# Scan stage of a hybrid decoder layer: the old sample states turned and multiplied ahead of the unit loop

## Chip, cores and metric

One core of one Trainium2 chip runs the whole layer in one launch. The metric is the device time of one execution in microseconds; given is the median of three runs. The instructions are put on five engines by hand: TensorE (PE), VectorE (DVE), ScalarE (ACT), GpSimd (POOL) and SyncE (SP), which here issues the loads and stores of the stage. Each engine works through its own list in order and waits on semaphores.

## What is computed

A layer over one prompt of 512 tokens and eight samples of 8 tokens each: latent attention, a state-space scan, a merge, and a mixture of experts. The change is in the scan. Of the reference:

```python
a_cs = jnp.cumsum(dt * a, axis=2)
cb = jnp.einsum('bclgn,bcsgn->bclsg', cm, bm)
w_ls = cb[..., None] * decay_ls * dt[:, :, None]
y_diag = jnp.einsum('bclsgh,bcsghp->bclghp', w_ls, x)
states = jnp.einsum('bclgn,bclgh,bclghp->bcghpn', bm, decay_end * dt, x)
def step(h, inp):
    s_c, d_c = inp
    return d_c[..., None, None] * h + s_c, h
y_off = jnp.einsum('bclgn,bcghpn->bclghp', cm, h_prev) * jnp.exp(a_cs)[..., None]
```

The prompt starts from a zero state; each sample starts from its own old state (32 heads of 64 by 128 numbers), which gives a part of its outputs (`y_off`), is aged by the decay over its 8 tokens, and gets a new part added (`states`). Everything is float32.

## The kernel before

The scan, `stage_ssd`, stands between the convolution and the merge; stages end in a barrier of all engines. It has G = 4 groups of 8 heads (512 columns, GW) and in each group NT = 5 units: four of 128 prompt tokens, the fifth with all 64 sample tokens. That makes N = 20 units k = 5g + i.

Ahead of the loop come the step sizes and decays (VectorE and ScalarE, L1595 to L1633), their cumulative sums on TensorE (L1397 to L1403), and a round trip of rows through device memory (L1341, L1342), from which `decays(k)` (L1326) loads the rows that unit k needs, three units ahead.

TensorE's list in turn k of the loop (L1515) is: `inputs(k)` (transposes L1417, then b and c.b, L1423 and L1424), `gate(k-1)` (eight products of 128x512 with the z weights, L1443), `turn(k-2)` (transposes of a finished y, L1512), `outputs(k-1)` (eight head products L1455, the product with the prompt's state L1458, the new state L1461). VectorE's list in its turn k is: copy b, mask c.b, subtract (L1654), minimum (L1656), after ScalarE's exponential the product L1659; then for unit j = k-1 the scaling L1670, three sums and products into y, the prompt state's update (L1685, L1687), and the norm (L1704).

In a sample unit `outputs` has more. After transposing the finished prompt state (L1466), it takes the eight old states of the group in h0 (128 x 4 x 8 x 128) one by one: four transposes (L1480), ScalarE's copy to h0T (L1582), a product (L1489) of 64 masked columns c_of with it, all into PSUM bank 5, while VectorE ages h0 (L1668). Then eight products (L1498) of 64 rows make the new parts in two banks in turn, and VectorE adds each to h0 (L1694) before its bank is used again. The masked operands are made by GpSimd (L1386, L1389). SP loads h0 of a group with four transfers of 512 KB (L1320), stores it with four (L1334), and loads the next group's only when the stores have landed. It does so in one list with the decay rows, the z weights (L1315) and the norm's gains (L1337).

## Time and profile before

| | us |
|---|---|
| runs: median (lowest to highest) | 2748.0 (2741.38 to 2751.46) |
| profiled execution, device time | 2731.32 |
| profiled execution, span of the trace | 2729.6 |
| busy over the span: TensorE | 2533.2 (93%) |
| VectorE | 1860.1 (68%) |
| ScalarE | 1345.2 (49%) |
| GpSimd | 482.8 (18%) |
| mean granted TensorE clock | 0.955 of full speed |

Busy times are those of the profiled execution, in which matmul ends are modelled. Work is named by the line of the kernel that issues it. A float32 product stands in the trace as two records, and a transpose as one. PEclk is the share of full speed that was granted: 1.00 is 2.4 GHz, 0.50 is 1.2 GHz. In brackets behind a row of a timeline stands how long the engine had been idle, and what released it.

### The profile page before, as it was taken

The page shows a single profiled execution, that of the slowest core. Times are in us where ns is not written, and L with a number is a line of the kernel's source. Part 1 is how long each engine was busy: PE and PEld are TensorE (multiplying, and loading weights), DVE is VectorE, ACT ScalarE, POOL GpSimd, SP SyncE. Part 2 cuts the span into 40 slices and gives each one's busy share as a digit, 9 for nine tenths or more (in the row PEclk, how much of TensorE's full clock was granted, in tenths as well). Part 3 has the DMA queues.
Part 4 walks back from the last instruction along what each step waited for, and adds up shares of the span by engine and source line. Part 5 has one row for each costly group of instructions (what it writes and reads, how often), then busy time and mean ns, then how long its engine had stood idle before and what let it go on. Part 6 is the DMA issues. An engine that isn't in the chain of part 4 may idle for free. (4 is left out here: it accounts for less than half of the span.)

```text
span 2729.6 us, 35842 instructions
## 1 busy us (share of the span) xinstructions
PE 2533.2 (93%) x13071; PEld 1934.0 (71%) x13071; DVE 1860.1 (68%) x2181; ACT 1345.2 (49%) x1412; POOL 482.8 (18%) x332
## 2 busy tenths in 40 slices
PE   8798999798995999979978899999999999999996
PEld 5355555598993444439976788888888888888882
DVE  0344444333775666653456799999999999999996
ACT  0243323132333454433122577777777777777771
POOL 0001122000001333210010721122222222122220
PEclk9899999899997898889988999999999999999998
DMA  4102344132214124213250899999999999999985
GB/s 145 69 1 99 117 157 171 35 93 68 78 62 140 58 94 131 83 50 86 84 200 27 302 408 401 384 379 386 383 378 381 378 380 377 380 384 378 379 338 197
DMA packets 239605, 589.63 MB, mean 216 GB/s; under 512 B 21680, under 2 KB 110992, under 8 KB 235024
## 3 DMA queue, kind: packets, MB, share of 16 engines
q1 hardware_dynamic: 222328, 512.09, 51.7%
q0 software_dynamic: 17168, 76.05, 7.3%
q8 instruction: 73, 1.20, 0.2%
q14 instruction: 36, 0.29, 0.0%
HBM read 555.18 MB, written 32.78 MB: 215 GB/s over the span
## 5 line engine op out<-in xcount | busy, mean ns | idle before, releaser
L2419 DVE TENSOR_TENSOR w_lo<-w_raw,w_hi 128x2048 fp32r<-128x2048 f32 x291 | 664.2, 2293 | 64.7 <-ACT w_hi L2372 63.0
L2372 ACT ACTIVATE w_hi<-w_raw 128x2048 fp32r<-128x2048 f32 x288 | 552.3, 1918 | 144.7 <-PE banks L2291 117.5
L2291 PE MATMUL banks<-w_hi,x_hi 128*128 128x512 f32 x1024 | 320.0, 394 | 3.6 <-DVEq L2458 2.0
L2291 PE MATMUL banks<-w_lo,x_hi 128*128 128x512 f32 x1024 | 316.9, 391 | 0.0
L2291 PE MATMUL banks<-w_hi,x_lo 128*128 128x512 f32 x1024 | 316.1, 390 | 0.0
L2419 DVE TENSOR_TENSOR w_lo<-mergedT,w_hi 128x2048 fp32r<-128x2048 f32 x96 | 220.7, 2299 | 23.1 <-ACT w_hi L2372 23.1
L2291 PEld LDWEIGHTS banks<-w_hi,x_lo 128*128 128x128 f32 x1024 | 192.8, 188 | 41.0
L2291 PEld LDWEIGHTS banks<-w_lo,x_hi 128*128 128x128 f32 x1024 | 192.9, 188 | 40.7
L2291 PEld LDWEIGHTS banks<-w_hi,x_hi 128*128 128x128 f32 x1024 | 190.5, 189 | 41.9 <-DVEq L2458 2.0
L2372 ACT ACTIVATE w_hi<-mergedT 128x2048 fp32r<-128x2048 f32 x96 | 184.1, 1918 | 49.1 <-PE banks L2291 42.7
L2250 POOL DMA_INDIRECT y_rows<-xT,to_row x33 | 52.3, 1585 | 818.9 <-ACT xT L2402 817.7
L2291 PE MATMUL banks<-w_hi,h_hi 128*128 128x512 f32 x512 | 158.3, 390 | 0.0
L2291 PE MATMUL banks<-w_hi,h_lo 128*128 128x512 f32 x512 | 158.0, 390 | 0.0
L2291 PE MATMUL banks<-w_lo,h_hi 128*128 128x512 f32 x512 | 157.8, 389 | 0.0
L1443 PE MATMUL banks<-wz,xT 128*128 128x512 f32 (+1 forms) x320 | 144.8, 606 | 1.5 <-ACT zs L1558 1.5
L2291 PEld LDWEIGHTS banks<-w_hi,h_hi 128*128 128x128 f32 x512 | 96.0, 188 | 20.9 <-DVE h_lo L2423 0.4
L2291 PEld LDWEIGHTS banks<-w_lo,h_hi 128*128 128x128 f32 x512 | 96.1, 188 | 20.6
L1443 PEld LDWEIGHTS banks<-wz,xT 128*128 128x128 f32 (+1 forms) x320 | 57.5, 185 | 74.9 <-issue 74.4
L2291 PEld LDWEIGHTS banks<-w_hi,h_lo 128*128 128x128 f32 x512 | 96.1, 188 | 20.2
L1381 POOL TENSOR_TENSOR xdt<-xs_t,dt 128x512 f32<-128x512 f32 (+1 forms) x20 | 26.1, 1303 | 420.8 <-ACT xs_t L1548 420.8
L1025 PE MATMUL banks_a<-part_hi_a,w_mhi_a 128*128 128x288 f32 x384 | 83.2, 298 | 14.2 <-DVE w_mlo_a L1061 14.2
L2236 POOL DMA_INDIRECT xT<-h_rows,from_row x32 | 83.8, 2619 | 28.6 <-POOL from_row L2232 27.8
(469 smaller groups left out, 4762.3 us busy)
## 6 DMA issues: line engine op xcount, KB each, us to landing
w_raw<-in_exp_w_gu SPq DMA_DIRECT2D x196, 1024.0 KB, 7.6
w_raw<-in_exp_w_down SPq DMA_DIRECT2D x96, 1024.0 KB, 5.9
mergedT<-in_exp_w_gu SPq DMA_DIRECT2D x64, 1024.0 KB, 7.4
mergedT<-in_exp_w_down SPq DMA_DIRECT2D x32, 1024.0 KB, 6.6
w_x<-in_w_in SPq DMA_DIRECT2D x11, 1024.0 KB, 5.2
out<-h SPq DMA_DIRECT2D x20, 512.0 KB, 4.7
wz<-in_w_in SPq DMA_DIRECT2D x4, 2048.0 KB, 10.4
dec<-acs_rows SPq DMA_DIRECT2D x16, 512.0 KB, 3.9
```

The lines of the kernel that those rows point to most:

```text
L1025: mm = pe.matmul(bank_of(u)[:, piece], wp[:, u % NW, k, :], part[:, piece * H2:(piece + 1) * H2], start=(k == 0 and wp is w_hi and n == 0) ...
L1381: ins = pool.tensor_tensor(heads(o[0:n, k % 2], n), x, f[:, g * HG:(g + 1) * HG].unsqueeze(2).broadcast_to((n, HG, PD)), ALU.mult)
L1443: mm = pe.matmul(banks[0:n, 7, :], sb.xT[:, q, P * i:P * i + n], wz[:, g % 2, q, :], start=(q == 0), stop=(q == KD - 1))
L2236: pool.indirect_dma_start(out=x_raw, out_offset=None, in_=io.h_rows, in_offset=bass.IndirectOffsetOnAxis(ap=from_row[:, par, :].bitcast(U3 ...
L2250: pool.indirect_dma_start(out=io.y_rows, out_offset=bass.IndirectOffsetOnAxis(ap=to_row[:, par, :].bitcast(U32), axis=0), in_=y_out, in_of ...
L2291: mm = pe.matmul(banks[:, bank + c, :], x[:, k, :], part[:, s % NHI, j, c * 512:(c + 1) * 512], start=start, stop=last)
L2372: act.activation(w_hi[:, s % NHI], raw(s, par), ACT.Copy).then_inc(hi_ready, 1)
L2419: dve.tensor_tensor(w_lo[:, s % NHI], raw(s, par), w_hi[:, s % NHI].bitcast(F32), ALU.subtract).then_inc(lo_ready, 1)
```

## The change

All 32 old states are now loaded once ahead of the unit loop, by halves of a group (`half_states`, four transfers of 256 KB each) that alternate between the two halves of h0, in front of, between and behind the loads that SP had there. TensorE takes them in 16 pairs: `turn_pair` transposes two samples' states into two banks, ScalarE (`old_copy`) and VectorE (`old_put`) copy one each, and `old_outputs` multiplies them with the masked c: the first sample of a pair goes to PSUM partitions 0 to 63, the second to 64 to 127, summed over the four pairs of a group. ScalarE copies the upper half out and VectorE adds both into old_y. The cumulative sums (`decay_sums`) come after the eighth pair. `seq_decays` makes the 32 heads' sample decays in one go after the first inputs; they were made per group (L1430, L1646).

The group's h0 is loaded a second time for the new states, as before. Its ageing is four instructions over 128x1024, two in the third and two in the fourth unit of the group, ahead of that unit's y; old_y is scaled in the fourth. The eight new-state products stand one behind each of the eight gate products of the sample unit, with 32 rows each: b_of has half its width, and the two halves of the rows hold samples 0 to 3 and 4 to 7. They go to banks 2 and 3. VectorE's additions (`add_new`) stand behind the next unit's minimum, or at the start of the last turn. The sample unit's `outputs` is left with its head products and the transposes of the prompt state. Buffers: h0T now lies in xdt and xend, c_of has two buffers, old_y is new. Each diff line below is cut from the full diff, whose renamings and semaphore counts are left out.

```diff
+        t1, t2, t3 = (y[:, 0, j * NT * SH:(j + 1) * NT * SH].rearrange("p (i h) -> p i h", i=NT) for j in range(3))
+        h0T = [t[:, j, :] for t in (xdt, xend) for j in range(2)]
+        uppers = [zs[0:NS, :], off[0:NS, :]]
+        old_y = buf("old_y", [NS, G, GW])
...
-        c_of = buf("c_of", [P, NSEQ, NS])
-        b_of = buf("b_of", [NS, NSEQ, NST])
-        e_seq = buf("e_seq", [P, 4, NSEQ])
+        c_ofs = [buf(f"c_of{j}", [P, NSEQ, NS]) for j in range(2)]
+        b_of = c_ofs[1][0:NS].rearrange("p b n -> p (b n)").rearrange("p (b n) -> p b n", b=NSEQ // 2)
+        e_seq = buf("e_seq", [P, G, 4, NSEQ])
...
+                def last_state(g):
                     sp.wait_ge(fin_out, g + 1)
                     sp.dma_start(io.o_ssmp[g * GW:(g + 1) * GW, :].rearrange("(q p) n -> p q n", p=P), st_out[:]).then_inc(p_out, 16)
+
+                def new_states(g):
                     sp.wait_ge(hs_out, 8 * (g + 1))
...
+                def half_states(c):
+                    g, half = divmod(c, 2)
+                    if c >= 2:
+                        sp.wait_ge(hT_ready, 2 * (c - 1))
+                    for q in range(4):
+                        at = g * GW + q * P
+                        sp.dma_start(h0[:, q, 4 * half:4 * half + 4], io.ssm[4 * half:4 * half + 4, at:at + P, :].rearrange("b p n -> p b n")).then_inc(half_in[half], 16)
+
+                for c in range(2):
+                    half_states(c)
                 z_weights(0)
+                for c in range(2, 6):
+                    half_states(c)
                 sp.wait_ge(rows_out, 1)
                 sp.dma_start(io.acs_rows[0:4 * SH, :], acsT[:, 0, :]).then_inc(rows_in, 16)
                 sp.dma_start(io.acs_rows[4 * SH:5 * SH, 0:NS], acsT[0:SH, 1, 0:NS]).then_inc(rows_in, 16)
                 sp.wait_ge(rows_in, 32)
                 for k in range(3):
                     decays(k)
+                for c in range(6, 8):
+                    half_states(c)
                 z_weights(1)
+                sp.wait_ge(hT_ready, NP)
                 old_states(0)
...
             def _(pool):
+                for g in range(G):
+                    if g >= 2:
+                        pool.wait_ge(off_part, PAIRS * (g - 1))
+                    pool.tensor_tensor(c_ofs[g % 2][:], sb.xbcT[:, 20 + g, SEQ:T].unsqueeze(1).broadcast_to((P, NSEQ, NS)),
+                                       K[:, K_BCOL:K_BCOL + NSEQ * NS].rearrange("p (b n) -> p b n", b=NSEQ), ALU.mult).then_inc(c_put, 1)
...
                     if i == NT - 1:
                         if g >= 1:
                             pool.wait_ge(hs_ready, 8 * g)
-                        pool.tensor_tensor(c_of[:], sb.xbcT[:, 20 + g, SEQ:T].unsqueeze(1).broadcast_to((P, NSEQ, NS)),
-                                           K[:, K_BCOL:K_BCOL + NSEQ * NS].rearrange("p (b n) -> p b n", b=NSEQ), ALU.mult)
                         pool.wait_ge(cb_out, k + 1)
-                        pool.tensor_tensor(b_of[:], b_t[0:NS, k % 2, :].unsqueeze(1).broadcast_to((NS, NSEQ, NST)),
-                                           K[0:NS, K_BROW:K_BROW + NSEQ].unsqueeze(2).broadcast_to((NS, NSEQ, NST)), ALU.mult).then_inc(of_seq, 1)
+                        many = (NS, NSEQ // 2, NST)
+                        pool.tensor_tensor(b_of, b_t[0:NS, k % 2, :].unsqueeze(1).broadcast_to(many),
+                                           K[0:NS, K_BROW:K_BROW + NSEQ // 2].unsqueeze(2).broadcast_to(many), ALU.mult).then_inc(of_seq, 1)
...
+                def seq_decays():
+
+                    pe.wait_ge(prep_a, 4)
+                    for h in range(SH):
+                        q, half = h // 2, PD * (h % 2)
+                        e_h = e_end[0:NS, NT - 1, h:h + 1].broadcast_to((NS, PD))
+                        mm = pe.matmul(banks[half:half + PD, 3, q * NSEQ:(q + 1) * NSEQ], e_h,
+                                       K[0:NS, K_BEND:K_BEND + NSEQ], start=True, stop=True)
+                    mm.then_inc(e_ready, 1)
...
+                def turn_pair(v):
+
+                    g, p = divmod(v, PAIRS)
+                    pe.wait_ge(half_in[v // 2 % 2], 64 * (v // 4 + 1))
+                    if v >= 2:
+                        pe.wait_ge(hT_out, v - 1)
+                        pe.wait_ge(hT_put, v - 1)
+                    for j in range(2):
+                        for q in range(4):
+                            mm = pe.transpose(banks[:, TURN + 2 * (v % 2) + j, q * P:(q + 1) * P], h0[:, q, 2 * p + j, :], K[:, K_ID:K_ID + P])
+                    mm.then_inc(hT_ready, 1)
...
+                def old_outputs(v):
+
+                    g, p = divmod(v, PAIRS)
+                    pe.wait_ge(hT_out, v + 1)
+                    pe.wait_ge(hT_put, v + 1)
+                    if p == 0:
+                        pe.wait_ge(c_put, g + 1)
+                        if g >= 2:
+                            pe.wait_ge(old_sum, g - 1)
+                    for j in range(2):
+                        mm = pe.matmul(banks[j * NS:(j + 1) * NS, SUM + g % 2, :], c_ofs[g % 2][:, 2 * p + j, :], h0T[2 * (v % 2) + j],
+                                       start=(p == 0), stop=(p == PAIRS - 1))
+                    mm.then_inc(off_part, 1)
...
+                def new_states(g, u):
+
+                    q, half = divmod(u, 2)
+                    if u == 0:
+                        pe.wait_ge(of_seq, g + 1)
+                        pe.wait_ge(e_out, 1)
+                    if 8 * g + u >= 2:
+                        pe.wait_ge(hs_out, 8 * g + u - 1)
+                    k = NT * g + NT - 1
+                    rows = slice(32 * half, 32 * half + 32)
+                    pe.matmul(banks[:, 2 + half, :], xend[rows, k % 2, q * P:(q + 1) * P], b_of[rows], start=True, stop=True).then_inc(hs_ready, 1)
...
-                    if g >= 1 and i == 0:
-                        pe.wait_ge(hs_out, 8 * g)
+                    else:
+                        pe.wait_ge(old_sum, G)
                     for q in range(KD):
                         mm = pe.matmul(banks[0:n, 7, :], sb.xT[:, q, P * i:P * i + n], wz[:, g % 2, q, :], start=(q == 0), stop=(q == KD - 1))
-                    mm.then_inc(z_ready, 1)
+                        if q == KD - 1:
+                            mm.then_inc(z_ready, 1)
+                        if i == NT - 1:
+                            new_states(g, q)
...
                         if g >= 1 and i == 0:
-                            pe.wait_ge(hs_out, 8 * g)
+                            pe.wait_ge(fin_out, g)
...
+                    mm.then_inc(y_ready, 1)
                     pe.wait_ge(st_new, NT * (g + 1))
                     for q in range(4):
                         mm = pe.transpose(banks[:, 6, q * P:(q + 1) * P], stT[:, q * P:(q + 1) * P], K[:, K_ID:K_ID + P])
                     mm.then_inc(fin_ready, 1)
-                    pe.wait_ge(h_in, 64 * (g + 1))
-                    pe.wait_ge(of_seq, g + 1)
...
-                    turn_state(0)
-                    for b in range(NSEQ):
-                        m = NSEQ * g + b
-                        if b + 1 < NSEQ:
-                            turn_state(b + 1)
-                        pe.wait_ge(hT_out, m + 1)
-                        mm = pe.matmul(banks[0:n, 5, :], c_of[:, b, :], h0T[:, b % 2, :], start=(b == 0), stop=(b == NSEQ - 1))
-                        mm.then_inc(off_part, 1)
-                        if b == NSEQ - 1:
-                            pe.wait_ge(off_part, m + 1)
-                            pe.sem_inc(y_ready, 1)
-                    for u in range(8):
-                        q, half = divmod(u, 2)
-                        if u >= 2:
-                            pe.wait_ge(hs_out, 8 * g + u - 1)
-                        mm = pe.matmul(banks[:, 6 + u % 2, :], xend[0:n, k % 2, q * P:(q + 1) * P], b_of[:, 4 * half:4 * half + 4, :],
-                                       start=True, stop=True)
-                        mm.then_inc(hs_ready, 1)
-                    pe.wait_ge(hs_ready, 8 * g + 8)
-                    pe.sem_inc(st_ready, 1)
...
+                def decay_sums():
+
+                    pe.wait_ge(prep_v, 6)
...
+                    mm.then_inc(sums_ready, 1)
+
+                turn_pair(0)
+                for v in range(NP):
+                    if v + 1 < NP:
+                        turn_pair(v + 1)
+                    old_outputs(v)
+                    if v == NP // 2 - 1:
+                        decay_sums()
+                pe.wait_ge(sums_out, 1)
+                pe.wait_ge(rows_out, 1)
...
+                def old_copy(v):
+
+                    act.wait_ge(hT_ready, v + 1)
+                    if v >= 2:
+                        act.wait_ge(off_part, v - 1)
+                    act.activation(h0T[2 * (v % 2)], banks[:, TURN + 2 * (v % 2), :], ACT.Copy).then_inc(hT_out, 1)
+                    if v >= 1 and v % PAIRS == 0:
+                        upper_half(v // PAIRS - 1)
+
+                def upper_half(g):
+
+                    act.wait_ge(off_part, PAIRS * (g + 1))
+                    if g >= 2:
+                        act.wait_ge(old_sum, g - 1)
+                    act.activation(uppers[g % 2], banks[NS:2 * NS, SUM + g % 2, :], ACT.Copy).then_inc(half_out, 1)
...
+                for v in range(NP // 2 + 1):
+                    old_copy(v)
...
+                for v in range(NP // 2 + 1, NP):
+                    old_copy(v)
+                upper_half(G - 1)
...
-                            for b in range(NSEQ):
-                                m = NSEQ * g + b
-                                act.wait_ge(hT_ready, m + 1)
-                                if m >= 2:
-                                    act.wait_ge(off_part, m - 1)
-                                act.activation(h0T[:, b % 2, :], banks[:, 7 - b % 2, :], ACT.Copy).then_inc(hT_out, 1)
...
+                def add_new(g):
+
+                    dve.wait_ge(aged, 2 * (g + 1))
+                    for u in range(8):
+                        q, half = divmod(u, 2)
+                        dve.wait_ge(hs_ready, 8 * g + u + 1)
+                        old = h0[:, q, 4 * half:4 * half + 4, :].rearrange("p b n -> p (b n)")
+                        dve.tensor_tensor(old, old, banks[:, 2 + half, :], ALU.add).then_inc(hs_out, 1)
+
+                def old_put(v):
+
+                    dve.wait_ge(hT_ready, v + 1)
+                    if v >= 2:
+                        dve.wait_ge(off_part, v - 1)
+                    dve.tensor_copy(h0T[2 * (v % 2) + 1], banks[:, TURN + 2 * (v % 2) + 1, :]).then_inc(hT_put, 1)
+                    if v >= 1 and v % PAIRS == 0:
+                        add_halves(v // PAIRS - 1)
+
+                def add_halves(g):
+
+                    dve.wait_ge(half_out, g + 1)
+                    dve.tensor_tensor(old_y[:, g, :], uppers[g % 2], banks[0:NS, SUM + g % 2, :], ALU.add).then_inc(old_sum, 1)
...
+                for v in range(NP // 2 + 1):
+                    old_put(v)
...
+                for v in range(NP // 2 + 1, NP):
+                    old_put(v)
+                add_halves(G - 1)
...
                         dve.tensor_scalar(seg, seg, 0.0, None, ALU.min).then_inc(seg_out, 1)
+                        if k >= 1 and unit(k - 1)[1] == NT - 1:
+                            add_new(unit(k - 1)[0])
...
+                        if k == 0:
+                            dve.wait_ge(e_ready, 1)
+                            dve.tensor_copy(e_seq[:].rearrange("p g q b -> p (g q b)"), banks[:, 3, 0:G * 4 * NSEQ]).then_inc(e_out, 1)
+                            dve.wait_ge(e_out, 1)
+                    else:
+                        add_new(G - 1)
...
                         hs = slice(g * HG, (g + 1) * HG)
-                        if i == NT - 1:
-                            for b in range(NSEQ):
-                                dve.wait_ge(hT_ready, NSEQ * g + b + 1)
-                                dve.tensor_tensor(h0[:, :, b, :], h0[:, :, b, :], e_seq[:, :, b:b + 1].broadcast_to((P, 4, NST)), ALU.mult).then_inc(aged, 1)
+                        if i in (2, 3):
+                            dve.wait_ge(h_in, 64 * (g + 1))
+                            for q in (2 * (i - 2), 2 * (i - 2) + 1):
+                                ins = dve.tensor_tensor(h0[:, q], h0[:, q], e_seq[:, g, q].unsqueeze(2).broadcast_to((P, NSEQ, NST)), ALU.mult)
+                            ins.then_inc(aged, 1)
+                        if i == NT - 2:
+                            dve.wait_ge(old_sum, G)
+                            dve.tensor_tensor(heads(old_y[:, g, :], NS), heads(old_y[:, g, :], NS), e_acs[0:NS, NT - 1, hs].unsqueeze(2).broadcast_to((NS, HG, PD)),
+                                              ALU.mult).then_inc(old_scaled, 1)
                         dve.wait_ge(y_ready, j + 1)
-                        dve.tensor_tensor(heads(off[0:n], n), heads(banks[0:n, 5, :], n), e_acs[0:n, i, hs].unsqueeze(2).broadcast_to((n, HG, PD)),
-                                          ALU.mult).then_inc(y_step, 1)
-                        dve.wait_ge(y_step, 2 * j + 1)
+                        if i < NT - 1:
+                            dve.tensor_tensor(heads(off[0:n], n), heads(banks[0:n, 5, :], n), e_acs[0:n, i, hs].unsqueeze(2).broadcast_to((n, HG, PD)),
+                                              ALU.mult).then_inc(y_step, 1)
+                            dve.wait_ge(y_step, 2 * j + 1)
+                            earlier = off[0:n]
+                        else:
+                            dve.wait_ge(old_scaled, g + 1)
+                            dve.sem_inc(y_step, 1)
+                            earlier = old_y[:, g, :]
...
-                        else:
-                            for u in range(8):
-                                q, half = divmod(u, 2)
-                                dve.wait_ge(hs_ready, 8 * g + u + 1)
-                                old = h0[:, q, 4 * half:4 * half + 4, :].rearrange("p b n -> p (b n)")
-                                dve.wait_ge(aged, NSEQ * (g + 1))
-                                ins = dve.tensor_tensor(old, old, banks[:, 6 + u % 2, :], ALU.add)
-                                ins.then_inc(hs_out, 1)
-                            if g + 1 < G:
-                                dve.memset(stT[:], 0.0).then_inc(st_new, 1)
+                        elif g + 1 < G:
+                            dve.wait_ge(fin_ready, g + 1)
+                            dve.memset(stT[:], 0.0).then_inc(st_new, 1)
```

## Rows read from the trace of the kernel before

**Rows 1.** Table of stretches: length, busy us (count) by engine, PEclk, DMA share, GB/s.

```profile
1009.00:1022.00 13.00, 12.63 (x48) 4.88 (x48) 5.54 (x8) 5.44 (x10) 0.00 (x0) 1.00 0.00 0
1026.00:1036.00 10.00, 10.00 (x12) 3.14 (x10) 3.48 (x6) 0.90 (x1) 0.00 (x0) 0.50 0.01 2
1136.00:1144.00 8.00, 8.00 (x40) 5.15 (x40) 4.12 (x7) 2.51 (x5) 0.00 (x0) 1.00 1.06 296
524.00:538.00 14.00, 13.22 (x61) 13.03 (x62) 2.73 (x8) 0.00 (x0) 0.00 (x0) 0.50 0.00 0
834.00:1223.00 389.00, 346.06 (x1290) 173.37 (x1290) 235.11 (x365) 169.60 (x245) 102.72 (x68) 0.89 0.31 94
```

**Rows 2.** Timeline of PE, second group's sample turn and first's: start, us, operation [idle before].

```profile
906.07 0.60 PE L1417 MATMUL banks<-const,xbcT 128*128 128x128 f32 x4
...
946.75 1.09 PE L1417 MATMUL banks<-const,xbcT 128*128 128x128 f32 x4 [0.30 <-PE banks L1498]
...
985.45 0.63 PE L1430 MATMUL banks<-const,e_end 64*64 64x8 f32 x16
...
996.93 0.60 PE L1417 MATMUL banks<-const,xbcT 128*128 128x128 f32 x4
...
997.79 7.08 PE L1443 MATMUL banks<-wz,xT 128*64 128x512 f32 x16
...
1006.46 0.66 PE L1466 MATMUL banks<-const,stT 128*128 128x128 f32 x4
...
1017.78 0.66 PE L1480 MATMUL banks<-const,h 128*128 128x128 f32 x4
...
1018.37 1.07 PE L1489 MATMUL banks<-h0T,c_of 128*64 128x512 f32 x2
...
1019.37 0.66 PE L1480 MATMUL banks<-const,h 128*128 128x128 f32 x4
...
1025.50 10.60 PE L1498 MATMUL banks<-b_of,xend 64*128 64x512 f32 x12 [1.51 <-DVE h L1694]
...
1036.41 1.09 PE L1417 MATMUL banks<-const,xbcT 128*128 128x128 f32 x4 [0.30 <-PE banks L1498]
```

**Rows 3.** Timeline of DVE, second group.

```profile
982.04 1.23 DVE L1659 TENSOR_TENSOR dec<-dec,cb 128x1024 f32<-128x1024 f32 x1 [1.12 <-ACT dec L1550]
...
983.70 0.69 DVE L1670 TENSOR_TENSOR off<-banks,e_acs 128x512 f32<-128x512 f32 x1 [0.43 <-PE banks L1458]
...
996.27 0.69 DVE L1670 TENSOR_TENSOR off<-banks,e_acs 128x512 f32<-128x512 f32 x1 [1.14 <-PE banks L1458]
...
1002.30 0.29 DVE L1643 COPY b_t<-banks 128x128 f32<-128x128 f32 x1
...
1004.40 1.42 DVE L1656 TENSOR_SCALAR dec<-dec 128x1024 f32<-128x1024 f32 x1
...
1029.32 0.69 DVE L1694 TENSOR_TENSOR h<-h,banks 128x512 f32<-128x512 f32 x1 [1.02 <-PE banks L1498]
```

**Rows 4.** Timeline of PE in the attention over sample keys.

```profile
401.70 1.94 PE L687 MATMUL banks<-keyT,qlS 128*64 128x512 f32 x8
```

**Rows 5.** Timelines of SP, PE and DVE, opening of the scan stage.

```profile
850.77 0.33 SPq L1341 DMA_DIRECT2D acs_rows<-st_out  x1
...
852.63 1.28 SPq L1326 DMA_DIRECT2D dec<-acs_rows  x3
...
861.68 1.89 PE L1455 MATMUL banks<-xdt,dec 128*128 128x64 f32 x16
...
875.17 0.83 DVE L1704 SCALAR_TENSOR_TENSOR y<-y,ssq,gn 128x512 f32<-128x512 f32 x1 [3.13 <-DMA gn<-in_ssd_norm_g]
```

**Rows 6.** Timelines of PE and SP, last group and end of the stage.

```profile
1176.90 7.08 PE L1443 MATMUL banks<-wz,xT 128*64 128x512 f32 x16
...
1213.72 3.99 SPq L1334 DMA_DIRECT2D out<-h  x4
...
1223.73 9.66 SPq L1007 DMA_DIRECT2D w_raw_a<-in_w_in  x4
```

115 lines of the change are left out of this document (51 added, 64 removed).

## The prediction, made before the changed kernel was seen

> **What bounds the kernel now.** First the table of stretches. The scan stage runs from 834 to 1223 us, the stages meet at barriers of all engines, so a microsecond won or lost here is one of the whole. TensorE is busy for 346.06 of its 389 us [rows 1]: it is the bound, and what the change moves must be read as TensorE time, waits of TensorE, or clock. Next its own timeline, in the second group (one turn of the unit loop starts where L1417 does) [rows 2]. The turn before it, in which L1430 stands 0.9 behind the start at 985.45, takes 12.4 us: gate products 7.1, the rest transposes and the unit's own products. The turn from 996.93 to 1036.41 takes 39.5 us, because after the last prompt states are turned (L1466, 1006.46 + 0.66) come the eight old states, transposed and multiplied, to about 1022, and eight new-state products, to 1036. The first group's turn takes 40.7 (906.07 to 946.75) [rows 2]. Third the clock column: TensorE is granted 2.4 GHz (1.00) through 1009 to 1022, and 1.2 GHz (0.50) through 1026 to 1036 [rows 1]. Before it fell, TensorE had stood idle for 1.5 us of waits on VectorE's additions [rows 2], and while it was at 1.2 GHz it ran 64-row products back to back without the clock coming back. The 14 us at 524 to 538 are the same: busy 13.22, clock 0.50 all the way [rows 1].
>
> Last VectorE, since the additions sit there. It is 60% busy over the stage [rows 1] but a chain: its wait before L1670 is 0.43 us in the third unit of a group and 1.14 in the fourth [rows 3]. That is all the slack before the places where the change puts new work.
>
> **Removed, per group.** From 1007.1 (end of the prompt state's transposes) to 1036.41, 29.3 us: the old states and new states of the turn. In the first group 30.5.
>
> **Added between the gates, per group.** Eight products of 32 rows by 512 columns alternate with the eight gate products of the sample unit. The trace has no 32-row product. A gate product at 2.4 GHz takes 7.08/8 = 0.88 us, a 64-row product at 1.2 GHz 1.70 us (the additions L1694 follow each other so) [rows 2, 3]. I take 0.86 and 1.71 for a product at the two levels; fewer rows don't shorten the streaming of 512 columns, and I see nothing cheaper than 0.86. Each change between shapes costs something too: four transposes and one 128x64 product recur every 1.59 us (1017.78 to 1019.37), of which 0.44 and 0.86 are work, so 0.15 per change (the product itself begins 0.59 behind the transposes' start) [rows 2]. One step, gate or product with its change, is 1.0 us at 2.4 GHz and 1.87 at 1.2.
>
> The third product waits for the first addition (L1694's work, now in VectorE's `add_new`), and that stands behind the next unit's subtraction and minimum. Before, the minimum ends at 1004.40 + 1.42 = 1005.8 [rows 3]. The ageing of h0, two instructions of 128x1024 in each of the third and fourth units, comes ahead of those; the nearest row is 1.23 each (L1659) [rows 3]. Third unit: 2.46 - 0.43 of slack = 2.0 late, which reaches TensorE's next input transposes as 1.7 (they wait for ScalarE's copy behind it). Fourth unit: 2.46 + 0.69 for the scaling of old_y - 1.14 leaves 2.0 more, less 0.2 for the dropped e_seq copy: 3.8. So the first addition is done at 1005.8 + 3.8 + 0.7 = 1010.3. TensorE starts the gate at 997.79 + 1.7 = 999.5, does five steps by 1004.5 and then stands for 5.8 us. Queued behind it: six products, five gate products, turn, the unit's outputs. The remaining eleven steps take 11.0 us at 2.4 GHz, or 20.6 at 1.2.
>
> With 2.2 us for what follows (1004.8 to 1007.1 before), the next turn starts at 1010.3 + 11.0 + 2.2 = 1023.5 against 1036.41: 12.9 won at full clock. At 1.2 GHz it is 1010.3 + 20.6 + 3.5 = 1034.4: 2.0 won. The first group wins 1.2 more either way. In the last group there is no next unit: VectorE's addition comes 3.5 us sooner (1002.3 to 1005.8 falls away) and the gate 0.9 sooner, so the stall is 3.2. From the gate's start to the first store of h0 today are 36.8 us (1176.90 to 1213.72), and 10.0 more to the next stage's first load (1223.73) [rows 6], which stay. New, the store waits for the prompt state's copy: 1.7 + 5.0 + 3.2 + 11.0 + 2.2 + 0.8 = 23.9, so 12.9 won, or 2.0 at 1.2 GHz. Four groups: **54 us at full clock, 9 at 1.2 GHz** (14.1 + 3 x 12.9 = 52.8, and 0.8 as the turns behind start at full clock; 3.2 + 3 x 2.0 = 9.2).
>
> Which clock? The stall of 5.8 us is longer than the idle before the fall today, so it falls. Behind it come alternating 128x64 and 32-row products. The nearest rows are the 64-row products of 1026 to 1036, unbroken at 1.2 GHz [rows 1]; half of the new stream has still fewer rows. I take 1.2 GHz for all eleven steps. The Trainium skill (TensorE: Matmul & The Clock Gate, Part 1) says "the default state is throttled, and activity releases the throttle"; by that rule unbroken products would bring it back, which the stretch 1026 to 1036 speaks against. It is a rival below.
>
> **Added ahead of the units.** All 32 old states are read once more: 8.4 MB. The stretch 1136 to 1144, mostly such loads, moves 296 GB/s [rows 1]: 28.3 us. The Trainium skill (DMA: Bandwidth & Descriptors, section Bandwidth) gives 341 GB/s for 1 MB; by that it would be 24.6 and the sum 4 lower.
>
> In SP's order the first two half-groups stand ahead of z_weights(0), the next four ahead of the decay rows, two behind decays(0) to (2). TensorE per pair: eight transposes 0.87, two products on the two column halves. Four such products (eight records, L687) take 1.94 us [rows 4], so a pair takes 0.95; with two changes a pair is 2.1 us at 2.4 GHz, 4.0 at 1.2. ScalarE and VectorE copy one half each beside it (0.69 for 512 columns, L1670) [rows 3]. Half-groups of 1 MB are 3.5 us of queue, and each waits until the one two before is turned, then 1.3 for its start, an estimate below the 1.9 in which a small write lands in rows 5.
>
> Step by step, the first load is issued a little behind the stage's start at 834, and I put its data, behind three small broadcasts, at 838.5: half-groups land at 842, 846, then 2 MB of wz, 855, 858, 863, 867. After the eighth pair, at 865, come the cumulative sums (3.3), at 869 the rows go out. Today that is 850.77, and 1.9 later (852.63) the decays are issued [rows 5]; so 872 for the decays, 5.2 us of queue, and the last half-groups land at 881 and 885. TensorE finishes the last pairs by 893, the half sums by 894. Then the first inputs 0.9, 32 small products of seq_decays 2.3 (eight are busy for 0.63, the last overlapping the next product) [rows 2], inputs 0.9, the first gate 7: the first unit's own products start at 904.5 against 861.68 [rows 5]: **+43**. Bounds: 33 if TensorE is never late and the queue never empty, 53 with the clock half the time at 1.2 GHz. In return VectorE's 3.1 us wait for the norm gains (875.17) [rows 5], queued behind h0 and wz today, is gone, as they land long before: -3.
>
> Edits at nothing: c_of on GpSimd moves to the start, under the loads; b_of is half as large, there before the gate. The new_states stores wait less for VectorE and h0's reload (2 MB) has two units of cover before the ageing; if that cover goes, each microsecond counts, since SP's decays stand behind it.
>
> **Sum.** +43 - 3 - 9 = +31 us on the profiled execution: 2731.32 (span 2729.6) becomes 2762. The shown runs have their median at 2748.0, 17 above; the difference carries over, so 2779.
>
> **Rivals.**
> 1. The clock returns a few us after the stall. Each group loses 2.5 of its 13: 44 won. +40 - 44 = -4: 2744. For it: in the same stage 128x64 products with transposes run at 1.00 [rows 1, 2]. Against: rows 1's two stretches.
> 2. The clock never falls in the gates and the opening runs at its queue bound: 40 - 9 - 54 = -23, 2725. It needs the additions to come before TensorE has stood long; the slack in rows 3 speaks against it.
> 3. The opening stays at 1.2 GHz, being broken by waits for loads: 16 pairs of 4.0 us are 64 from 846, 21 later than above (64 + 3.3 for the sums, against 893 - 846 = 47): 2800. Decides from where TensorE's pair (4.0) is slower than the queue's half (3.5 for two pairs). Against: full 128-row products and transposes, unbroken in that case.
> 4. The halves of a pair don't run side by side: 0.9 us more a pair, partly under the loads, some 6 more: within the range; rows 4 speak against it.
>
> **Chances.** Forecast 0.5 (2769 to 2789 by the opening's bounds), rival 1 0.3 (2734 to 2754), rival 2 0.15, rival 3 with 4 0.05. A measurement of this kernel tells about 0.5%, 13.7 us, from no change. Faster: rival 2 and a sixth of rival 1 (which ends at the bound), 0.20. Same: most of rival 1 and the low edge of the forecast, 0.27. Slower: 0.53. The range 2728 to 2797 leaves out half of rival 2 and rival 3.
>
> **What would show it.** In the changed profile: unit products starting near 904; TensorE standing some 6 us before the third product, released by the addition; granted clock 0.50 to the end of the sample gate, and that gate some 30 us long in all; turns of prompt units still 12 to 13 us; the sample turn about 36 instead of 39.5 (and the one before it 1.7 longer). It is wrong if the gate's clock is 1.00 (rival 1 or 2), or if the opening is under 33 or over 53 us.

## The result and the profile after

| | before | after |
|---|---|---|
| median of 4 runs each, us | 2744.7 | 2782.7 |
| ratio, 95% interval | | 1.0137 (1.0116 to 1.0158) |
| profiled execution, us (its span) | 2731.3 (2729.6) | 2782.5 (2780.7) |
| scan stage, first load of it to first load of the next, us | 389.5 | 428.3 |
| its start to the first unit's products, us | 27.5 | 76.5 |
| turn of a sample unit, second group, us | 39.5 | 37.4 |

The change costs 38 us by the medians, and the scan stage is 38.7 us longer in the traces. It was forecast at +31. The two profiled executions are 51.1 us apart: 12.4 of that lie outside the stage, where the code is the same. Over the thirteen traces of this case the rest of the layer takes 2340 to 2352 us, shortest in the kernel before and longest in the changed one, so I compare stages below and not spans. Within the stage the phase ahead of the units costs 49 and the groups win 10.

The table of stretches of the changed kernel (columns as in [rows 1]): the whole stage, four stretches of the first group's sample turn, and one of the last group's gate.

```profile
840.75:1269.02 428.27, 368.85 (x1290) 174.78 (x1290) 246.04 (x366) 163.50 (x233) 114.07 (x68) 0.79 0.36 105
...
958.00:964.00 6.00, 5.98 (x17) 1.84 (x17) 5.86 (x9) 1.31 (x3) 1.32 (x1) 1.00 0.15 58
964.00:970.00 6.00, 0.03 (x1) 0.03 (x1) 5.02 (x9) 3.31 (x5) 4.53 (x3) 0.80 0.00 0
970.00:980.00 10.00, 10.00 (x11) 2.27 (x12) 2.01 (x4) 1.70 (x2) 0.22 (x1) 0.50 0.00 0
980.00:996.00 16.00, 16.00 (x40) 6.21 (x40) 5.00 (x7) 1.62 (x3) 0.00 (x0) 0.50 0.01 4
...
1232.00:1256.00 24.00, 24.00 (x44) 6.80 (x43) 4.18 (x7) 1.19 (x2) 0.00 (x0) 0.50 0.00 0
```

TensorE works through 958 to 964 at 2.4 GHz, stands for 6 us, and then is busy for every microsecond of the next 26 at 1.2 GHz: 21.5 us of the narrow products, then 4.5 of transposes and head products. Its timeline in the first group's sample turn, L1503 the gate, L1492 the new products; they are the counterpart of the 10.60 us of L1498 in [rows 2]:

```profile
957.91 0.63 PE L1438 MATMUL banks<-const,xbcT 128*128 128x128 f32 x4 [0.88 <-ACT xbcT L1642]
...
961.86 1.12 PE L1492 MATMUL banks<-c_of,xend 32*128 32x512 f32 x2
962.91 1.07 PE L1503 MATMUL banks<-wz,xT 128*64 128x512 f32 x2
969.97 2.07 PE L1492 MATMUL banks<-c_of,xend 32*128 32x512 f32 x2 [5.99 <-DVE h L1672]
971.97 1.97 PE L1503 MATMUL banks<-wz,xT 128*64 128x512 f32 x2
973.87 2.07 PE L1492 MATMUL banks<-c_of,xend 32*128 32x512 f32 x2
```

Steps start 1.00 to 1.05 us apart before the stall and 1.90 to 2.00 apart behind it. The second and third groups repeat it (6.00 us of stall in each). The clock comes back in the next unit's gate, whose products are 128x128x512, about 2 us into it here and 2.5 us in the second group (a timeline row of that gate, and two rows of the table):

```profile
996.82 7.81 PE L1503 MATMUL banks<-wz,xT 128*128 128x512 f32 x16
```

```profile
998.00:999.00 1.00, 1.00 (x3) 0.31 (x3) 0.00 (x0) 0.99 (x2) 0.00 (x0) 0.81 1.08 321
999.00:1000.00 1.00, 1.00 (x4) 0.45 (x3) 0.82 (x2) 0.98 (x3) 0.33 (x1) 1.00 1.04 289
```

VectorE over the time of the stall, the counterpart of [rows 3]:

```profile
965.81 0.28 DVE L1746 COPY b_t<-banks 128x128 f32<-128x128 f32 x1
...
966.21 1.67 DVE L1751 TENSOR_TENSOR dec<-dec,acs 128x1024 f32<-128x1024 f32 x1
967.91 1.42 DVE L1753 TENSOR_SCALAR dec<-dec 128x1024 f32<-128x1024 f32 x1
969.24 1.27 DVE L1672 TENSOR_TENSOR h<-h,banks 128x512 f32<-128x512 f32 x2
```

The first product has been ready since 961; the first addition stands behind the fourth unit's chain and the next unit's subtraction and minimum, and starts at 969.24. The phase, in SyncE's and TensorE's timelines, beside [rows 5]:

```profile
853.62 21.01 SPq L1356 DMA_DIRECT2D h<-in_state_ssm  x16
882.48 0.34 SPq L1364 DMA_DIRECT2D acs_rows<-st_out  x1
...
884.34 1.28 SPq L1335 DMA_DIRECT2D dec<-acs_rows  x3
885.67 9.19 SPq L1356 DMA_DIRECT2D h<-in_state_ssm  x8
```

```profile
862.56 1.97 PE L1465 MATMUL banks<-const,h 128*128 128x128 f32 x8 [3.18 <-DMA h<-in_state_ssm]
...
875.52 1.97 PE L1465 MATMUL banks<-const,h 128*128 128x128 f32 x8 [1.94 <-DMA h<-in_state_ssm]
...
895.95 1.97 PE L1465 MATMUL banks<-const,h 128*128 128x128 f32 x8 [6.23 <-DMA h<-in_state_ssm]
...
917.22 1.89 PE L1518 MATMUL banks<-xdt,dec 128*128 128x64 f32 x16
```

TensorE waits for half loads at 849.91 (the first), 862.56, 875.52 and 895.95, and the pairs behind these waits start at 1.2 GHz (1.97 for eight transposes, against 1.09); the first unit's products follow at 917.22.

### The profile page after: what moved, and what is told of

Read it like the earlier page. It is cut to its first block and busy times, and to the rows that moved or that the text cites. A ratio compares the mean times of both kernels' runs of the same rounds, so it can differ in the third digit from the quotient of the medians.

```text
span 2780.7 us, 35861 instructions
## 1 busy us (share of the span) xinstructions
PE 2562.9 (92%) x13071; PEld 1940.0 (70%) x13071; DVE 1872.3 (67%) x2182; ACT 1338.7 (48%) x1400; POOL 486.5 (17%) x332
## 5 line engine op out<-in xcount | busy, mean ns | idle before, releaser
L1503 PE MATMUL banks<-wz,xT 128*128 128x512 f32 (+1 forms) x320 | 169.5, 672 | 0.4 <-ACT zs L1635 0.4
L1503 PEld LDWEIGHTS banks<-wz,xT 128*128 128x128 f32 (+1 forms) x320 | 57.2, 194 | 93.7 <-issue 93.1
L775 DVE COPY keyT<-banks 128x512 f32<-128x512 f32 x96 | 63.0, 687 | 38.7 <-PE banks L650 33.0
```

Source lines behind the costliest of these rows:

```text
L775: dve.tensor_copy(keyT[:, s % 2, t, :], bank_of(u)).then_inc(bank_free[u % NB], 1)
L1503: mm = pe.matmul(banks[0:n, 7, :], sb.xT[:, q, P * i:P * i + n], wz[:, g % 2, q, :], start=(q == 0), stop=(q == KD - 1))
```

## The experiments

Theory A: the groups lose because the first addition is late, TensorE stands, its clock falls and the narrow stream behind doesn't bring it back; and the phase is a chain of half buffer freed, load, turn. Against it: that the narrow stream alone holds the clock down (theory B of the first runs), and that the queue's bytes bound the phase. Times are medians, or the time of a single run where the text says so. The kernel before gave 2738 to 2739 us beside these runs and 2744.7 beside the changed kernel. Expectations that start from the changed kernel's 2783 us (that of the run without the phase also from 2744.7) stand some 6 us too high against what was measured here; ratios and stages are free of that. The code cuts are shortened.

**The additions paced.** VectorE's eight additions are spread so that each stands where its product is ready:

```diff
 y = y * zs                 (turn before, fourth unit)
+add_new(g, (0, 1))
 ...
+add_new(g, (2, 3))         (head of the turn)
 b_t, cb, seg - own
+add_new(g, (4, 5))
 min(seg, 0)
-add_new(g)
+add_new(g, (6, 7))
```

> The changed kernel, with the eight additions of the new states moved on VectorE: two behind the gating product of the turn before, two at the head of the turn, two behind the subtraction and two behind the minimum, so that each stands where its product comes ready. Nothing is left out. Theory A (the stall of 5.99 us before the third product lets the clock fall, and it then stays at 1.2 GHz): without the stall the clock is 1.00 through all sixteen steps, a step is 1.03 us to the end, the turn around the products goes from 37.4 us to about 20 (6.0 of stall and eleven steps at 0.92 each saved), and the kernel comes to 2783 - 3 x 16 - 12 = about 2723 us. Theory B (the stream of 32-row products holds the clock down by itself): the clock falls near the same place, only the 6 us of stall go in three groups and 2 in the last, about 2763 us. Theory C (VectorE is late elsewhere by as much): no change, 2783 us.

Measured 2708.6 us, 0.988 of before (0.9835 to 0.9925). The stall before the third product is gone in all four groups, and the fall of the clock in three. Its table of stretches and, in the last group, its timeline of TensorE:

```profile
952.00:958.00 6.00, 6.00 (x14) 1.45 (x12) 5.86 (x9) 2.01 (x3) 0.58 (x1) 1.00 0.03 14
958.00:964.00 6.00, 6.00 (x13) 1.45 (x12) 4.90 (x10) 1.97 (x3) 4.30 (x3) 1.00 0.00 0
...
1160.00:1164.00 4.00, 4.00 (x5) 0.91 (x6) 3.65 (x7) 2.20 (x4) 0.00 (x0) 0.51 0.00 0
```

```profile
1155.83 1.04 PE L1503 MATMUL banks<-wz,xT 128*64 128x512 f32 x2 [0.39 <-ACT zs L1635]
1157.78 1.12 PE L1492 MATMUL banks<-c_of,xend 32*128 32x512 f32 x2 [0.91 <-POOL c_of L1423]
...
1161.59 1.97 PE L1503 MATMUL banks<-wz,xT 128*64 128x512 f32 x2
```

The sample turns take 19.5 us instead of 37.4 (951.17 to 970.64), sixteen steps of 1.03 us. Theory A holds for them, and B falls: the same 32-row stream ran 16 us at 2.4 GHz, three times. The last group won only 1.5 us; there the clock fell behind waits of 0.39 and 0.91 us that no addition causes. The stage is 62.7 us shorter than the changed kernel's (365.6 against 428.3), where theory A had 60; the median lies 14 us under A's number, 6 of them by the start named above and others by the spread of these runs, on which more below.

**Two additions early.** Only `add_new(g, (0, 1))` is moved, the other six stay behind the minimum.

> As the run with the paced additions, but only the first two additions are moved (behind the gating product of the turn before); the other six stay behind the minimum of the next unit. The wait moves from the third product to the fifth and is some 3 us instead of 6. Theory A, if any stall of some us lets the clock fall: clock 0.50 from the fifth product on, steps 1.95 us, saved 3 us of stall and two steps at 0.92, turn about 32.5 us, kernel about 2764 us. If 3 us of idleness leave the clock up: turn about 23 us, kernel about 2728 us. Theory B (the product stream alone): the clock falls at the same time as in the changed kernel, before the wait begins.

Measured 2733.5 us in a single run. The stall is 2.44 us and stands before the fifth product:

```profile
960.17 1.12 PE L1492 MATMUL banks<-c_of,xend 32*128 32x512 f32 x2
964.74 1.12 PE L1492 MATMUL banks<-c_of,xend 32*128 32x512 f32 x2 [2.44 <-DVE h L1673]
967.68 2.07 PE L1492 MATMUL banks<-c_of,xend 32*128 32x512 f32 x2
```

The clock falls with 2.44 us of idleness in all three groups: one step behind it in the first, within the step in the second (1.45 us), by its end in the third. Turns are 29.2 to 30.2 us. The kernel is 30 us under my number because the turns gained 7 to 8 us each instead of 5, because in the last group the clock stayed at 1.00 (products at 1.12 us to the last, against 2.07), 15 us more, and by the 6 us of the start. In that last group the waits of 0.39 and 0.90 us are there as in the others, and the clock did not fall.

**The stall filled.** VectorE's order is the changed kernel's; TensorE passes the wait with throwaway products:

```diff
+    if u == 2:
+        pe.wait_ge(y_step, 2 * (NT * g + NT - 1))
+        for _ in range(6 if g + 1 < G else 2):
+            pe.matmul(banks[:, 5, :], identity, xT[:, 0, 0:512])
     pe.wait_ge(hs_out, 8 * g + u - 1)
```

> The changed kernel with its VectorE order untouched: the additions come as late as before, but TensorE passes the wait of 5.99 us before the third product with six throwaway products of 128 rows and 512 columns (two in the last group), whose results nobody reads. Nothing else changes. It parts idleness from lateness. Theory A1 (what lets the clock fall is that TensorE stands idle): the third product still starts some 12 us into the turn, but the clock stays at 1.00, ten to eleven steps take 1.03 instead of 1.95 us, turn about 27 us instead of 37.4, kernel about 2783 - 3 x 10 - 9 = 2743 us. Theory A2 (the narrow stream behind it, 32-row products between gate steps of 64 columns, lets it fall a few us later whatever came before): clock 0.50 by the fifth step behind the filler, turn over 33 us, kernel 2765 us or more.

Measured 2740.8 us in a single run, near A1's 2743, but that is partly chance: the turns won 2, 12 and 3 us where A1 had 10 each, the last group 11. In the three groups 0.65 us of idleness is left behind the filler. The second group's turn was 25.5 us, at 1.00 throughout; the first and third were 35.1 and 34.8, the clock falling two to three steps on:

```profile
1041.34 5.42 PE L1491 MATMUL banks<-xT,const 128*128 128x512 f32 x12
1047.41 1.12 PE L1496 MATMUL banks<-c_of,xend 32*128 32x512 f32 x2 [0.65 <-DVE h L1676]
...
1057.68 1.12 PE L1496 MATMUL banks<-c_of,xend 32*128 32x512 f32 x2
...
1202.18 2.48 PE L1491 MATMUL banks<-xT,const 128*128 128x512 f32 x4
1204.59 1.12 PE L1496 MATMUL banks<-c_of,xend 32*128 32x512 f32 x2
```

In the last group the clock had fallen before the filler (a gate step of 1.97 at 1200.28), and two full products later the steps were at 1.12 again and stayed. So the clock came back within two full products where, in the changed kernel, 21.5 us of unbroken narrow ones did not bring it back. Neither A1 nor A2 is right as stated: with most of the idleness filled the clock stayed in one group and fell in two. That a narrow stream bears less idleness than a wide one fits the early phase, where waits of 2.02 and 2.08 us between pairs (in the best kernel and in the one with two additions early) left the clock at 1.00; but behind 1.94 us in the changed kernel's phase it fell, so this is not shown.

**The gate ahead.** TensorE's order alone: six gate steps where the stall was, the last six products behind them.

```diff
     for q in range(KD):
         gate step q
-        if sample unit: new_states(g, q)
+        if sample unit and q < 2: new_states(g, q)
+    if sample unit: for u in range(2, 8): new_states(g, u)
```

> The changed kernel with another order on TensorE alone: the gate's eight steps stand in front, the first two products still between them, and the other six products behind the eighth gate step. The VectorE order is untouched. Six gate steps of 0.88 us, 5.3 us, now lie where the stall of 5.99 us was. Theory A (idleness of some us lets the clock fall): under 1 us of idleness is left at the third product, the clock stays at 1.00 but for short waits for the additions, the products end some 17 us earlier, turn about 21 us, kernel about 2783 - 3 x 16 - 12 = 2723 us. Theory B (a run of six products of 32 rows, with a short wait of each for an addition, is too thin to hold the clock): the clock falls among the last products, turn 24 to 27 us, kernel about 2745 us.

Measured 2721.4 us, 0.9932 of before (0.9912 to 0.9952). The wait before the third product is 1.71 us, not under 1, and the clock falls within some 2 us behind it; turns of 23.3 to 23.6:

```profile
961.73 1.72 PE L1492 MATMUL banks<-c_of,xend 32*128 32x512 f32 x4 [1.71 <-DVE h L1675]
```

```profile
961.00:964.00 3.00, 2.09 (x5) 0.96 (x6) 2.38 (x5) 2.86 (x3) 0.97 (x1) 0.90 0.00 0
964.00:969.00 5.00, 4.82 (x8) 1.61 (x7) 1.87 (x4) 0.07 (x1) 0.00 (x0) 0.50 0.00 0
```

That is my B for the turn, 24 to 27, undercut slightly: with only six products behind the fall little is left to run slow. The kernel came at A's time all the same: three turns won 14 us each, and the last group 10.5 (gate's start to its first store: 35.4 in the changed kernel, 24.9 here), a little less than the 12 expected; the phase, untouched, was 3.4 shorter in this execution.

**The phase left out.** No old state is turned, the early half loads are gone, `old_y` is set to zero.

> The changed kernel with its phase ahead of the units left out: no old state is turned or multiplied there, the early loads of half states are gone, and the old states' part of the sample outputs is zero (that part of the computation is left out). It prices the phase and the groups apart. By the prediction's sum (the phase +43 against the kernel before, the groups -12): 2744.7 - 12 = about 2733 us. By the trace of the changed kernel (first unit's products 49 us later, groups -10): 2782.7 - 49 = about 2734 us. Rival (the early phase also delays or speeds the groups by its state loads and buffers): the groups' turns differ from 12.5 and 37.4 us, and the time is off 2734 by more than 5 us.

Measured 2733.7 us in a single run. Both sums had that number, but from 2744.7 and 2782.7, and the kernel before gave 2738 here, so the hit is partly chance; the stage says more. Sample turns 37.42 us each, with the same stall of 6.00: the rival falls, phase and groups don't touch each other. Its stage takes 382.9, so the phase by itself costs 45.4. Its first unit's products stand 32.5 behind the stage's start, 5 later than in the kernel before. TensorE waits for no load there; the 32 small products of `seq_decays` take 3.6 us at 1.2 GHz, and the first gate takes 8.9 us instead of 7.0:

```profile
855.02 3.59 PE L1440 MATMUL banks<-const,e_end 64*64 64x8 f32 x64
...
860.09 8.89 PE L1491 MATMUL banks<-wz,xT 128*128 128x512 f32 x16
```

**The sums early.** `decay_sums()` and its copies behind the fourth pair instead of the eighth.

> The changed kernel with the decay sums, and the copies that follow them, moved from behind the eighth pair to behind the fourth, where TensorE waits 3.18 us for a load. Nothing is left out. Theory A (the phase is bound by the chain in which TensorE's late ninth and tenth pair and the decay rows hold back the issue of the last half loads): the last halves are issued some 4 to 6 us earlier, the wait of 6.23 us before the thirteenth pair shrinks to under 2, and the kernel gains 4 to 6 us: about 2778 us. Theory B (the phase is bound by the queue that brings 8 MB of states): the wait moves to another pair, no change, 2783 us.

Measured 2779.3 us, 1.0142 of before (1.0125 to 1.0159), not to be told from the changed kernel. The phase takes 78.1 us (76.5 before the edit), and the last wait is 7.80 instead of 6.23:

```profile
874.11 0.52 SPq L1364 DMA_DIRECT2D acs_rows<-st_out  x1
874.67 0.43 SPq L1365 DMA_DIRECT2D acs_rows<-st_out  x1
878.68 1.28 SPq L1335 DMA_DIRECT2D dec<-acs_rows  x3
```

The rows needed 3.6 us to land (878.68 less 875.10) instead of 1.1; they now stood right behind the sixth half load. The decays were issued 44.2 us behind the stage's start, against 43.6 in the changed kernel: what was won on TensorE was lost in the queue. Theory A failed here, but B is not shown either; that took two more orders.

**The gate's weights later.** `z_weights(0)` behind the sixth half load.

> The changed kernel with the first 2 MB of gate weights issued behind the sixth half load instead of behind the second. Nothing is left out. In the changed kernel these 2 MB pass the queue in front of the third half group, which TensorE then waits for, while the queue moves only 87 to 102 GB/s between 876 and 888 us. Theory A (the phase is a chain of half buffer freed, load, turn, and each load's landing carries to the end): the third half group lands up to 6 us earlier, the weights pass in the slack stretch, the phase is some 5 us shorter, kernel about 2778 us. Theory B (a later link, the rows and decays in front of the last half loads, holds the end whatever comes before): the waits move to a later pair, kernel 2783 us.

Measured 2775.6 us, 1.0139 of its before (1.0118 to 1.016), by the ratio not to be told from the changed kernel either. The wait of 3.18 is down to 0.67, the phase is 4.1 us shorter (72.4), of which 1.8 may be spread (below), but the last wait grew to 11.07: the rows took 5.4 us behind the weights' 2 MB. By the traces each theory had half of it; by the runs nothing was won.

**Paced and weights later together.**

> The paced additions and the later gate weights together, nothing left out. If both gains stand by themselves: the paced kernel's 2708.6 us less what the later weights give in the run by themselves (0 to 6 us), 2703 to 2709 us, 1.1 to 1.3% under the kernel before. If they share a cause: no better than the paced kernel.

Measured 2708.2 us, 0.9876 (0.9849 to 0.9904). No better than the paced kernel by the runs. In the traces the stage is 1.3 us shorter: 2.3 won in the phase, and 1.0 lost in the last group, where the clock fell one step sooner.

**A new order of the phase.** Sums behind the fourth pair, and in SyncE's queue:

```diff
-z_weights(0)
 half_states(2) ... half_states(5)
 rows out
+half_states(6)
 decays(0) ... decays(2)
-half_states(6)
 half_states(7)
+z_weights(0)
 z_weights(1)
```

> The changed kernel with another order in its early phase and nothing else: the decay sums stand behind the fourth pair, and SyncE issues the seventh half load ahead of the decays, the eighth behind them, and both gate weights last. Nothing is left out. In the runs with one of these alone the last wait of TensorE for a half load stayed (7.80 us with the sums early, 11.07 us with the weights later), and the phase, from the stage's start to the first unit's products, measured 78.1 and 72.4 us against 76.5. Theory A (the last link, decay rows and their way through a full queue ahead of the seventh half load, is what held the end): the last wait falls under 4 us, the first unit's products stand 64 to 67 us after the stage's start, kernel about 2772 us. Theory B (the queue's bytes bound it: 8 MB of states and 4 MB of weights at about 300 GB/s end 40 us after the start, and the last pairs with the gate follow): the gate's first 2 MB, now last, hold the first unit back instead, 72 us or more, kernel 2777 us or more.

Measured 2770.1 us, 1.011 (1.0086 to 1.0133). First unit's products 68.0 us after the stage's start, a little outside theory A's 64 to 67, last wait 3.81:

```profile
875.49 2.03 SPq L1356 DMA_DIRECT2D h<-in_state_ssm  x4
877.56 1.45 SPq L1335 DMA_DIRECT2D dec<-acs_rows  x3
880.23 3.97 SPq L1356 DMA_DIRECT2D h<-in_state_ssm  x4
884.25 4.18 SPq L1324 DMA_DIRECT2D wz<-in_w_in  x2
```

The weights last did not hold the gate, so B falls. How much the order gives needs the spread: in five kernels whose phase is the changed kernel's, the first unit's products stand 73.1 to 76.5 us after the start (median 74.7), in the three with the new order 65.5 to 68.0. So some 7 of the phase's 49 us were its order. Which of the three moves gave how much was not run. The rest are pairs, 8 MB of loads and the way from the last pair to the first unit.

**Both together, and the last group shifted.** First the paced additions with the new order; then, in the last group alone, each product one gate step later.

> The paced additions and the phase's new order together, nothing left out. Without the clock's fall a step of the groups costs 1.03 us, so both gains should add: the paced kernel's 2708.6 us less 8 to 12 us, 2697 to 2701 us, some 1.5% under the kernel before. If the phase's order gives nothing (theory B of the run with the order alone): 2704 us or more.

Measured 2705.5 us, 0.9874 (0.9848 to 0.99), over the 2697 to 2701 of the sum and where theory B had it: the medians of the two paced kernels differ by 3 us although the stage is 9.6 us shorter (356.0 against 365.6). The runs of the paced kernels scatter by some 20 us (2692 to 2712 here), and their mean granted clock, recorded for every run, orders them: the sixteen runs of the three of them that leave the last group as it was are at 0.958 to 0.963 and 2692 to 2703 us, or at 0.952 to 0.955 and 2701 to 2721. The medians mix the two sets in different shares. Within the lower clock they are 2719.8 (paced) and 2710.4 (both), 9.4 us apart as the stages are; within the higher one 2698.6 and 2695.2. The step between the sets, 15 to 21 us, is about what the last group loses when its clock falls (15.2, below); that this is what parts them is likely but not shown, as only one execution of each was traced.

> As the run with both, and in the last group alone the eight products stand one gate step later, so that the first of them no longer waits 0.91 us for the copies of B that GpSimd makes. The paced kernel's clock fell in this group (behind waits of 0.39 and 0.91 us) and not in the other three, which have no wait. Theory A (there the summed idleness of 1.3 us decides): with 0.4 us left the clock stays up, the thirteen slow steps take 1.03 us, 12 us less than the run with both, about 2688 us. Theory B (the narrow steps let it fall there anyway, since the turn has no full-width input products in front): no change against the run with both.

Measured 2692.3 us, **0.9831 of before (0.9807 to 0.9856)**, the lowest median of all. Its last group, a row of TensorE and two stretches:

```profile
1152.18 1.90 PE L1503 MATMUL banks<-wz,xT 128*64 128x512 f32 x4 [0.39 <-ACT zs L1640]
```

```profile
1152.00:1158.00 6.00, 5.78 (x12) 1.43 (x12) 5.90 (x9) 1.09 (x4) 2.07 (x1) 1.00 0.00 0
1158.00:1164.00 6.00, 6.00 (x13) 1.45 (x12) 4.55 (x9) 2.92 (x5) 0.00 (x0) 1.00 0.00 0
```

With 0.39 us of idleness in place of 1.30 the clock stays, and from the gate's start to the group's first store are 18.4 us instead of 33.6. The median is 13.3 us lower than the run with both, where theory A had 12; theory B falls. One trace alone would not say it, since the kernel with two additions early kept its clock in this group with 1.29 us of waits.

## Why the prediction held, and where it was off

**Direction and mechanism: right.** The stall, its length, its cause and the clock behind it came as worked out: 5.99 us against 5.8, released by the addition, granted clock 0.50 to the end of the gate, sample turn shorter than before by 2 us. The steps measured 1.03 and 1.95 us against 1.0 and 1.87. The length of the stall owes something to errors that cancel: the turn before grew by 0.5 us and not 1.7, and the addition was done about 3 us later than in the kernel before and not 3.8. The term for full clock was tested too: 998.6 to 1023.5, so 24.9 us for a turn with the late addition, and the second group of the filled kernel took 25.5.

**The phase: +49 against +43, the larger miss.** The step that failed is the way of a half load, "each waits until the one two before is turned, then 1.3 for its start". The sixth pair's transposes end at 868.3, the load that they release is there at 875.5: 7.2 us where 1.3 + 3.5 = 4.8 stood. The start fits (data moves from about 869.7 on); it is the 1 MB that took 5.8 us and not 3.5, its last part beside the sixth half load, issued at 872.6. From it the eighth pair, the sums and the rows slid from 35 to 41.7 us behind the stage's start. The stage began at 840.75 here and at 834.18 before, so that 917 against the forecast 904.5 is 6 us late and not 13. A second, smaller slip follows: from the decays' issue to the seventh half load 11.6 us and not 9. Over 842 to 908, while the old states came, 224 GB/s were moved on average and 321 at 870 to 871, so the bytes alone did not set the time. The bounds of 33 to 53 held. The profiled execution lies at the long end of the spread named above: by the median the phase cost 47. TensorE's clock fell at the waits and came back 3 to 6 us into the pairs behind them, which the forecast had only in its upper bound.

**The groups: -10 against -12 (3 of the norm gains' wait among them).** A sample turn is 37.4 where the forecast had 35.8: eleven slow steps took 21.5 and not 20.6, what follows them 3.9 and not 3.5, and the five steps and the stall ahead 0.2 more each. The turn before it grew by about 0.5 and not 1.7. The last group's stall before the third product is 2.10 and not 3.2, but 0.39 for ScalarE's gate copy and 0.91 for GpSimd's `b_of` come ahead of it; I had costed `b_of` (which the trace calls c_of, whose buffer it uses) at nothing, "half as large, there before the gate". In that group it isn't, and it takes longer than the whole did, in all four groups; the last, before and after:

```profile
1174.41 2.34 POOL L1389 TENSOR_TENSOR b_of<-b_t,const 64x1024 f32<-64x1024 f32 x1
```

```profile
1220.21 3.75 POOL L1423 TENSOR_TENSOR c_of<-b_t,const 64x512 f32<-64x512 f32 x1
```

The clock was already at 1.2 GHz at 1227.11, before the stall. So the last group won nothing: from its gate to the next stage's first load are 47.0 us (46.8 before, 44.8 forecast).

**The clock: the right level, but a cause told too simply.** I let the stall decide. It does for 6 us, always; for 2.4 us in three groups of three. But the clock also fell behind 1.3 us in two waits in the last group of ten of eleven kernels, and behind 0.65 in two groups of three, while with no wait inside the gate it never fell in twelve groups (each of these has 0.88 us of idleness at the head of its turn, in front of the full-width input products). So how much idleness is enough differs from case to case; whether the stream's width sets it is argued here, not shown. The Trainium skill (TensorE: Matmul & The Clock Gate, Part 1) says that activity releases the throttle; by the filled kernel's last group it does for full products (2.48 us of them), and by the changed kernel's 21.5 busy microseconds it does not for these narrow ones.

**The rivals.** Rival 2's first half (the additions come in time and the clock stays) is what the paced kernel was made into: its stage without the phase is 290.9 us (365.6 - 74.7) against 362.0 (389.5 - 27.5), 71 won where the rival had 54 and 3 for the norm gains, since the stall itself went too. Rival 1, the clock back after some us, was seen in no sample gate of the changed kernel. Rival 3 didn't come: the phase ran at 0.77 on average, a pair taking 2.03 us at 2.4 GHz and 3.80 at 1.2. Rival 4 neither: the two products of a pair take 1.08 us together at 2.4 GHz.

**The sum**: +31 forecast, +38.7 in the stage by the traces, 38.0 in the runs; 2779 against 2782.7. That the time is off by only 4 us is partly luck: the cost was 7 us too low, and the kernel before came out at 2744.7 and not at the 2748.0 from which I started.

## What to carry to other kernels

Interleaving work to fill an engine helps only if what the next step waits for on another engine has its place in that engine's order too; here four lines of VectorE's order decided between +38 and -30 us. Where a stream on TensorE is narrow, count every wait in it, the small ones of 0.4 and 0.9 us too, since the clock fell behind them in ten groups of eleven. Full products in the place of a wait can help (the filled kernel's last group won 11 us), but not surely (two of its other three groups won 2 to 3). A chain of double-buffered loads is priced from buffer freed to data there (7 us here for 1 MB, read once), not from bytes over bandwidth. Half the data can take longer, as `b_of` did: a term put at nothing wants a row.

## What the runs showed of the hardware

- Products of 32 rows alternating with 64-column gate products ran 16 us at a granted clock of 1.00 (paced) and 21.5 us at 0.50 (changed kernel), fully busy both times: without a wait in it, the stream kept the level that it found.
- The clock went from 0.50 to 1.00 within two full products of 128 rows (2.48 us) in one group of the filled kernel, and about 2 and 2.5 us into the gate of full products behind the changed kernel's first two sample turns. In the first gate of the kernel without the phase it took 3.7.
- The same wait doesn't always have the same effect: 0.65 us behind the same filler let the clock fall in two groups of three.
- A small write right behind a half load of 1 MB, and behind the weights' 2 MB, in the same queue took 3.6 and 5.4 us to land instead of 1.1.
- VectorE's scaling of 64x512 took 1.52 us in all four groups, where others of 512 numbers a row take 0.68; GpSimd's masking of the same shape took 3.75. They overlap in time, with each other or with the rest of VectorE's work, and no run parted the causes.
